# Value products of two tiles back to back in three attention stages of a one-core kernel

## What is computed

```
s = jnp.einsum('bqhd,bkhd->bhqk', q_block, k) * scale          # A: window of 3 blocks and 256 context keys
p = jax.nn.softmax(s (and a sink in A), axis=-1)
o = jnp.einsum('bhqk,bkhd->bqhd', p, v)                        # the value products
y = (o * jax.nn.silu(g)) @ w_o
```

## Time and profile before

| what | value |
|---|---|
| median of 3 runs | 1166.13 us (1163.79 to 1166.4) |
| the profiled execution: span | 1164.7 us, inside the range of the runs; the median is 1.4 us over it |
| stage A (attend) | about 106 to 403 us of the span |
| stage B (attend) | about 574 to 757 us |
| stage C (attend) | about 858 to 968 us |
| TensorE busy | 1102.9 us, 95% |
| VectorE, ScalarE busy | 726.2 us (62%), 652.1 us (56%) |
| DMA engines | 27.6% of their time |

### The profile page before, as it was taken

One profiled execution on the slowest core, in us unless ns is written; L12 is line 12 of the kernel. 1 busy time (PEld: TensorE's weight loads), 2 busy tenths in 40 slices (PEclk: granted clock), 3 DMA queues, 4 the chain that ended last, 5 costly groups with the idle time before them and its releaser, 6 DMA issues.

```text
span 1164.7 us, 20187 instructions
## 1 busy us (share of the span) xinstructions
PE 1102.9 (95%) x7408; PEld 899.2 (77%) x7408; DVE 726.2 (62%) x1584; ACT 652.1 (56%) x1363; POOL 416.5 (36%) x513
## 2 busy tenths in 40 slices
PE   4899999999998899999999999999999999999996
PEld 0587787878886589888688887798878777888785
DVE  5475665766668725463688788745766775427745
ACT  4614455545556525653577777846567753457733
POOL 1643112111220243676400001416653335456781
PEclk9899999999999999999999999999999999999999
DMA  8732343513113631131201101052312404213112
GB/s 353 270 144 64 111 171 104 187 64 145 46 28 122 228 105 37 37 108 38 57 10 37 64 10 36 13 164 72 87 37 87 150 19 127 91 55 117 47 37 73
DMA packets 34253, 109.33 MB, mean 94 GB/s; under 512 B 4516, under 2 KB 7076, under 8 KB 33772
## 3 DMA queue, kind: packets, MB, share of 16 engines
q1 hardware_dynamic: 34156, 108.05, 27.6%
HBM read 101.39 MB, written 2.11 MB: 89 GB/s over the span
## 4 chain that ended last, share of the span: by engine, by line
PE 77%; DVE 10%; ACT 5%; issue 3%; POOL 3%; DMA 2%; SPq 0%; POOLq 0%; DVEq 0%; ACTq 0%
PE PS L675 31%; PE PS L658 15%; PE PS L791 8%; PE PS L779 7%; PE PS L975 6%; PE PS L1043 3%; PE PS L710 2%; DMA AF<-wstream 2%; PE PS L876 1%; PE PS L691 1%; DVE AD L2364 1%; ACT AF L1267 1%; POOL AR L2545 1%; DVE AF L1982 1%; POOL AR L2561 1%
## 5 line engine op out<-in xcount | busy, mean ns | idle before, releaser
L2545 POOL TENSOR_TENSOR AR<-AF,AR 128x256 fp32r<-128x256 f32 x396 | 301.7, 797 | 596.3 <-ACT AR L1144 596.3
L675 PE MATMUL PS<-AR 128*128 128x512 f32 (+1 forms) x2208 | 450.4, 360 | 4.7 <-POOL AR L2545 1.4
L675 PEld LDWEIGHTS PS<-AR 128*128 128x128 f32 x2208 | 364.0, 189 | 71.8 <-issue 9.7
L658 PE MATMUL PS<-AR 128*128 128x256 f32 (+4 forms) x1284 | 245.5, 327 | 6.7 <-ACT AF L1267 1.7
L658 PEld LDWEIGHTS PS<-AR 128*128 128x128 f32 (+1 forms) x1284 | 180.3, 190 | 42.1 <-issue 21.7
L1276 ACT ACTIVATE AF<-PS 128x512 f32<-128x512 f32 (+3 forms) x192 | 124.6, 649 | 101.1 <-PE PS L779 97.0
L1267 ACT ACTIVATE AF<-PS,AF 128x512 f32<-128x512 f32 (+3 forms) x192 | 140.8, 734 | 27.1 <-DVE AF L2341 18.3
L779 PE MATMUL PS<-AF 128*128 128x128 f32 x864 | 127.7, 275 | 8.3 <-DVE AF L1982 5.7
L1144 ACT ACTIVATE AR<-AF 128x1024 fp32r<-128x1024 f32 x99 | 103.4, 1052 | 41.4 <-PE PS L975 27.9
L779 PEld LDWEIGHTS PS<-AF 128*128 128x128 f32 x864 | 100.2, 140 | 32.6 <-issue 15.5
L791 PE MATMUL PS<-AF 128*64 128x128 f32 x1728 | 115.8, 279 | 3.1 <-DVE AF L1989 2.2
(11 more groups left out here) (213 smaller groups left out, 1136.4 us busy)
## 6 DMA issues: line engine op xcount, KB each, us to landing
AF<-wstream SPq DMA_DIRECT2D x171, 512.0 KB, 5.1
AF<-x_in SPq DMA_DIRECT2D x2, 1024.0 KB, 8.9
AD<-rows SPq DMA_DIRECT2D x4, 512.0 KB, 5.8
out<-AF SPq DMA_DIRECT2D x16, 128.0 KB, 1.9
AF<-AF SPq DMA_DIRECT2D x28, 64.0 KB, 2.0
AF<-rpb_band SPq DMA_DIRECT2D x8, 224.0 KB, 4.9
BIAS<-rpb_band SPq DMA_DIRECT2D x8, 224.0 KB, 4.7
AF<-ctx_in SPq DMA_DIRECT2D x1, 1024.0 KB, 5.8
```

The costliest lines, as they stand in the source:

```text
L658: mm = pe.matmul(out, stationary, moving, start=i == 0, stop=i == len(products) - 1)
L675: mm = pe.matmul(out[:, 0:t1 - t0], a, b, start=k == 0 and i == 0, stop=k == nk - 1 and i == 2)
L2545: ins = pool.tensor_tensor(w[:, 1, at:at + 256], raw(c)[:, at:at + 256], w[:, 0, at:at + 256].bitcast(F32), ALU.subtract)
```

## The change

```diff
+                def weighed_at(m):
+
+                    due = m - behind - 1
+                    if not m0 <= due < m1:
+                        return []
+                    if due >= m1 - 2:
+                        return [due]
+                    return [due - 1, due] if (due - m0) % 2 else []
...
                         scores(2 * m)
+                    banks_read(m - behind == m0, 4, 5, 6)
+                    together = weighed_at(m)
+                    if len(together) == 2:
+                        for due in together:
+                            weigh_values(due)
                     if m0 <= m - behind < m1:
-                        banks_read(m - behind == m0, 4, 5, 6)
                         turn(2 * (m - behind))
-                    ahead = values_first or m == m1
-                    if ahead and m0 <= m - behind - 1 < m1:
-                        weigh_values(m - behind - 1)
+                    if m == m1 and len(together) == 1:
+                        weigh_values(together[0])
                     if m < m1:
                         banks_read(m == m0, 2, 3)
                         scores(2 * m + 1)
                     if m0 <= m - behind < m1:
                         turn(2 * (m - behind) + 1)
-                    if not ahead and m0 <= m - behind - 1 < m1:
-                        weigh_values(m - behind - 1)
-                    if m < m1 or values_first:
+                    if m > m1 and len(together) == 1:
+                        weigh_values(together[0])
+                    if m < m1 or fill_last:
                         for name in fillers(m):
                             make(name)
```

More of the change, by code:

```diff
@@ L794, in weigh_values, with attend @@
                 mm.then_inc(pv_done, 1)
-            def attend(m0, m1, pair_ready, fillers, behind=1, values_first=False, drained=True):
+            def attend(m0, m1, pair_ready, fillers, behind=1, fill_last=False, drained=True):
                 before = list(opened)
@@ L884, in ready_a @@
                     pe.wait_ge(kz_done, 2)
-            attend(0, A_END, ready_a, lambda m: fillers_a(m // 6 + 1, m % 6), values_first=True, drained=False)
+            attend(0, A_END, ready_a, lambda m: fillers_a(m // 6 + 1, m % 6), fill_last=True, drained=False)
             project("A.o0.0", "A.o0", OA, 0, H, k1=KD - 1)
```

## The result

The changed kernel takes 1192.93 us (median of 4 runs, 1191.0 to 1193.47) against 1164.96 for the one before (median of 4, 1162.9 to 1166.4): a ratio of 1.0239, with a 95% interval of 1.0224 to 1.0255, or 28 us slower. The forecast was 1185 us in a range of 1173 to 1196. The sign and the main mechanism held; 28 us came where 18.7 were forecast. Every run's time is some 1.8 us over its span. The profiled execution after, with 1189.2 us of span, is therefore the shortest of its four, and the one before, with 1164.7, the longest of its four, so the two profiles differ by 24.5 us and not by 28.

The account below looks back on a forecast made before the run. The prediction took TensorE to bound the kernel, busy 1102.9 of 1164.7 us. A +11, B +8.7 and C -1 sum to 18.7, giving 1183.4 on the profiled execution and 1184.8 as median, told as 1185, range 1173 to 1196.

Parts of the forecast that it names:

- The 17 us saved: All stages: 45 fewer groups of values save changes of form, A 8.7, B 5.7, C 2.7: 17.1 us if nothing waits.
- the first rival: All stages: the new waits stay hidden and only saved drains count, giving 1149 us; chance 0.05.
- 22.3 us were forecast for second turns: Stage A: without values between the turns, TensorE's second turn waits 0.26 to 0.71 us for ScalarE's copy, 22.3 in all.
- Some is absorbed. I take 2.5: Stage A: part of the added waits falls into TensorE's existing 12.1 us of idle time; 2.5 us taken, 0 to 8.
- the three shortages the first, 0.36 us: Stage B, behind the iteration with no filler: TensorE offers 3.57 us against a chain of 3.93, 0.36 short.
- The second, of ScalarE in the iteration with the filler of 0.70: Stage B: ScalarE needs 4.6 us against 4.27 offered, 0.35 short, up to 0.8 with accumulator reads and gaps.
- The third is right in its cause: Stage B, iteration with the 0.35 filler: VectorE needs 4.5 us and gets 3.92, 0.6 short, up to 2.
- the 1.8 taken: Stage B: added waits per pair of heads, 1.8 us from a range of 1.3 to 3.2; 14.4 for eight pairs.
- some 0.48 us too early for the copy, at some four places: Stage C: behind iterations without a filler values come 0.48 us before the copy is ready, some 1.7 us in all.
- the formula from A: Stage A: the second turn's wait for ScalarE's copy is 0.35 us plus the copy's time less the scores' time.
- The second, that B's engines run ahead: Stage B: ScalarE and VectorE use long iterations to run ahead, so only A pays: 1173 us; chance 0.17.
- The third, a falling clock: More waits bring more stretches of lower granted clock, each some 1.7 us; six would give 1195 us; chance 0.08.

Follow-up runs that it names:

- a_single_ahead: Changed kernel, but in A each tile's values alone ahead of the first turn, B and C as before: 1.0154 of the kernel before, A 310.91 us.
- a_only: The change (pairs ahead of the first turn) in stage A alone, B and C as before: 1.0128 of the kernel before, A 309.82 us.
- a_between_two: In A two tiles' values every second iteration, between first turn and second scores; B and C as before: 1.0059 of the kernel before, A 299.45 us.
- b_pair_early_gate: Pairs ahead of the first turn in B alone, with VectorE's gate one place earlier: 1.0074 of the kernel before, B 186.06 us.
- b_only: The change (pairs ahead of the first turn) in stage B alone, A and C as before: 1.0100 of the kernel before, B 190.72 us.
- a_fill_early: As a_between_two, with fillers between first turn and second scores in A's iterations without values: 1.0535 of the kernel before, A 354.52 us.
- b_single_ahead: In B each tile's values alone ahead of the first turn, A and C as before: 1.0113 of the kernel before, B 193.67 us.
- b_between_two: In B two tiles' values every second iteration, between first turn and second scores; A and C as before: 1.0125 of the kernel before, B 194.61 us.

## Why the prediction was right, and where it was off

**The prices of changing form: right.** 0.09 into the group from scores, 0.15 for the group and 0.05 for the turn behind it stand in the rows of B above. There are 50 groups instead of 95, as the order said. The 17 us saved are this price times the count; no run measures them as a whole. They fit what is seen: in A a_single_ahead, without them and with the same waits for the copy, is no faster than a_only although it has fewer other waits, and in B they close the sum of a pair of heads. By the rule of the Trainium skill that stood behind the first rival (TensorEngine Tiling (Array Packing), Key Properties) a change of mode drains the engine. The trace agrees that each change costs time, 0.34 us a group; as the waits came to more, this did not decide the sign.

**The copy in A: right to a hundredth of a microsecond in most tiles.** 22.3 us were forecast for second turns that wait for ScalarE's copy; the waits went from 1.1 to 22.6, by 21.5. The single waits over the six tiles of a pair are 0.25, 0.35, 0.46, 0.58, 0.70 and 0.49 us, where 0.26, 0.36, 0.46, 0.58, 0.71 and 0.49 were given. a_single_ahead and a_between_two show that they belong to the place.

**A's sum lacks a term: the filler's wait for bank 7.** The prediction added 22.3 for the copy, took off 2.5 as absorbed and 8.7 as saved, and put nothing down for fillers. The waits for VectorE ahead of them rose by 5 us, from 6.5 to 11.5. The prediction had looked at TensorE's existing idle time as room, and at buffers of the probabilities; it did not ask what the filler itself waits for. "Some is absorbed. I take 2.5" was about right: the idle times ahead of turns for divisions, of scores and of modulation rows for weights fell by 1.2, 1.1 and 0.6 us, 2.9 in all. With both, 21.5 + 5 - 2.9 - 8.7 = 14.9 us, where A came to +15.4 like for like (+13.9 between the two profiles, +15.8 in a_only) instead of +11.

**B: the direction right, the places mostly wrong, the size short.** Of the three shortages the first, 0.36 us behind the iteration with no filler, is there in size; but what comes late is the next scores, by 0.28 us for exponentials, and not the next turn. The second, of ScalarE in the iteration with the filler of 0.70, shows as no wait. The third is right in its cause: the iteration with the filler of 0.35 is too short for VectorE. "TensorE meets that at the next scores" named the wrong spot. What waits is that iteration's own filler, 1.34 us for bank 7, and its second turn, 0.38 more than before. At the stage's end scores wait twice more, 1.9 us in all. New waits are 24.6 - 23.3 + 0.7 = 2.0 us a pair of heads against the 1.8 taken, and with the end +11.9 or +11.3 over all instead of +8.7. That 1.8 came near 2.0 is in part luck, since most of it arises elsewhere. b_pair_early_gate settles that VectorE's queue ahead of the subtraction is what the filler waits for.

**C: wrong in sign, small.** The step "some 0.48 us too early for the copy, at some four places" had the right wait and too small a size: 1.4, 1.1 and 1.1 us at three places, because ScalarE has more in its queue before the copy than the formula from A has. That is 3.6 us against the 1.7 taken. C is +1.7 instead of -1, and some 0.8 us of the difference is not accounted for.

**The rivals.** The fast one fell with the bare waits in A. The second, that B's engines run ahead, fell with b_only (1.0100). The third, a falling clock, fell for this change: the windows after it have 1.00. In a_fill_early, where fillers and turns wait more, the clock did fall, to 0.95 over A. The Trainium skill, Perfetto Trace Analysis, Matmul Optimizations, says that it is "important that matmuls execute back-to-back in batches". These runs show that batching one kind of matmul is no gain by itself: batches of values left turns and fillers to wait, and the mean clock of A and B was 0.99 and 1.00 before and 1.00 after.

**What stays open.** The waits that make up the 6.6 us left in B after the earlier gate are read from the trace; no run takes one of them away. Whether a second bank for the fillers would turn the change into a gain was not tried, since all eight banks are in use in A and B.

## What to carry to other kernels

Work that looks like mere throughput may be the cover of a latency between its neighbours: before moving a group on an in-order engine, work out what the two instructions it stood between ask of each other, and what then fills the gap. Batching to save a fixed price makes rounds uneven; the engines that are even in mean then lag in the short rounds, and the first to feel it is whatever has a single buffer, here the filler's bank. Hold the saving, 0.34 us a group, against waits that a row of the old trace already shows bare: the one iteration without values had A's largest term.

## What was not expected

The values' place had a third function, seen only when it was changed alone: behind the second turn they left VectorE the time to free bank 6, and a wait of 1.65 us a pair of heads came out when they were moved one by one.

Stretches of a lower granted clock can't be read off the waits. In eight profiles A has its old order, and in all eight the scores near 326 us wait some 1.7 us for exponentials. In six of them a stretch at half the clock stands right behind that wait, as the 0.57 of the kernel before. In the other two, b_single_ahead and b_between_two, the wait is there, A has no such stretch, and one comes in B instead, at 752 and 731 us. The changed kernel waits more in all and has none in A, B or C; its window of the same times (some other place of its program, as it runs behind) reads:

```profile
327.00:331.00 4.00, 3.59 (x20) 3.06 (x20) 2.72 (x9) 2.74 (x8) 0.00 (x0) 1.00 0.00 0
```
